# TensorE's program written out for all heads of attention and mLSTM, and the mLSTM key turns set one projection unit ahead of their products

## What is computed

```python
kw = kc * wk
C_new = decay[..., None, None] * C + jnp.einsum('bshd,bshe->bhde', kw, vc)
n_new = decay[..., None] * n + jnp.sum(kw, axis=1)
```

## Time and profile before

| | |
|---|---|
| median of 3 runs | 3012.46 us (3005.94 to 3017.71) |
| the profiled execution | 3015.32 us, of it the span 3013.5 us |
| PE busy | 2774.6 us, 92% of the span, 16995 matmuls |
| DVE, ACT, POOL busy | 42%, 27%, 22% |
| attention phase on PE | about 124 to 1231 us |
| output projection of layer 0 | about 1246 to 1510 us |
| mLSTM heads | about 1512 to 2809 us, some 161 us each |
| final output | about 2813 us to the end |

### The profile page before, as it was taken

The page is one execution under the profiler, slowest core; times in us unless marked ns, Lnnn a source line. Parts: engine busy times, 40 slices in busy tenths (PEclk is TensorE's granted clock), DMA queues, the critical chain, the costliest instruction groups (busy, mean ns, idle before and its releaser), DMA issues. The chain is left out here.

```text
span 3013.5 us, 49037 instructions
## 1 busy us (share of the span) xinstructions
PE 2774.6 (92%) x16995; PEld 2349.4 (78%) x16995; DVE 1270.0 (42%) x3433; ACT 815.0 (27%) x2119; POOL 657.3 (22%) x815
## 2 busy tenths in 40 slices
PE   6789989999999899799799999999999999999898
PEld 3577777868777777588588888888889898888687
DVE  3536545472636365555403333241514142424633
ACT  3314423250524143222312212131313121222111
POOL 2421021103011211343101212030303031212532
PEclk9899999999999999799899999999999999999999
DMA  9411020203011111244102222121303121314443
GB/s 359 163 44 51 8 87 12 58 9 89 2 58 52 46 48 47 88 139 133 62 23 39 76 34 74 34 80 17 94 18 76 38 69 39 61 53 118 148 143 109
DMA packets 186555, 217.95 MB, mean 72 GB/s; under 512 B 26288, under 2 KB 133248, under 8 KB 184400
## 3 DMA queue, kind: packets, MB, share of 16 engines
q1 hardware_dynamic: 176336, 187.37, 21.7%
q10 hardware_dynamic: 9984, 27.37, 2.4%
HBM read 176.64 MB, written 38.07 MB: 71 GB/s over the span
## 5 line engine op out<-in xcount | busy, mean ns | idle before, releaser
L501 PE MATMUL psum<-h_hi,mlstm_w_lo 128*128 128x384 f32 (+1 forms) x1600 | 610.9, 382 | 33.6 <-issue 20.8
L502 PE MATMUL psum<-h_lo,mlstm_w_hi 128*128 128x384 f32 (+1 forms) x1600 | 579.2, 362 | 0.0
L503 PE MATMUL psum<-h_hi,mlstm_w_hi 128*128 128x384 f32 (+1 forms) x1600 | 578.3, 361 | 0.0
L501 PEld LDWEIGHTS psum<-h_hi,mlstm_w_lo 128*128 128x128 f32 x1600 | 305.4, 191 | 60.9 <-issue 31.7
L503 PEld LDWEIGHTS psum<-h_hi,mlstm_w_hi 128*128 128x128 f32 x1600 | 304.2, 190 | 28.8
L502 PEld LDWEIGHTS psum<-h_lo,mlstm_w_hi 128*128 128x128 f32 x1600 | 305.6, 191 | 21.0
L501 PE MATMUL psum<-h_hi,attn_w_lo 128*128 128x384 f32 (+1 forms) x800 | 293.8, 367 | 27.2 <-DVEq L779 12.3
L502 PE MATMUL psum<-h_lo,attn_w_hi 128*128 128x384 f32 (+1 forms) x800 | 290.6, 363 | 0.0
L503 PE MATMUL psum<-h_hi,attn_w_hi 128*128 128x384 f32 (+1 forms) x800 | 290.0, 362 | 0.0
L470 POOL CAST mlstm_w_hi<-mlstm_w_raw 128x512 fp32r<-128x512 f32 x78 | 47.9, 614 | 823.1 <-PE psum L503 757.5
L751 ACT ACTIVATE arena<-arena,negm 128x640 f32<-128x640 f32 (+2 forms) x208 | 161.8, 778 | 218.2 <-DVE negm L836 218.2
(11 more groups left out here) (276 smaller groups left out, 4898.4 us busy)
## 6 DMA issues: line engine op xcount, KB each, us to landing
m_bc<-gate_rows_mlstm SPq DMA_DIRECT2D x128, 256.0 KB, 3.8
mlstm_w_raw<-in_mlstm_w_in SPq DMA_DIRECT2D x40, 512.0 KB, 4.8
h_full<-gated_output SPq DMA_DIRECT2D x31, 512.0 KB, 4.1
arena<-in_rotary SPq DMA_DIRECT2D x24, 512.0 KB, 6.9
arena<-in_rotary SPq DMA_DIRECT2D x24, 384.0 KB, 3.7
gated_output<-gT SPq DMA_DIRECT2D x8, 1088.0 KB, 5.2
layer_output<-xb_out ACTq DMA_DIRECT2D x17, 512.0 KB, 2.6
h_hi_full<-layer_output SPq DMA_DIRECT2D x17, 512.0 KB, 4.7
```

Of the source, the lines that this page charges most:

```text
L501: pe.matmul(out, self.lo[:, k, :], E.h_hi[:, k, tok], start=(k == 0), stop=False)
L502: pe.matmul(out, self.hi[:, k, :], E.h_lo[:, k, tok], start=False, stop=False)
L503: ins = pe.matmul(out, self.hi[:, k, :], E.h_hi[:, k, tok], start=False, stop=(k == KT - 1))
```

## The change

Three things. TensorE's program for attention and for mLSTM is written out for all heads, so that no branch back and no wait against a register is left in it; the other engines keep their loops. The turn of a key tile and its products are put one projection unit apart: after unit i TensorE makes the products of tiles 2i-2 and 2i-1 and then turns tiles 2i and 2i+1, and ACT's copies follow in that order. And the two waits between the key units and the first query unit go behind that unit.

```diff
             def _(pe):
-                with pe.Fori(0, NKV) as kv:
+                for kv in range(NKV):
                     for m, kind in enumerate(kinds):
...
                         evac(NG + i)
-                        for c in (2 * i - 1, 2 * i):
+                        for c in (2 * i - 2, 2 * i - 1):
                             if 0 <= c < NT:
                                 act.wait_ge(s_kv, at(h * NT + c + 1))
...
-                    def key_step(s):
-
-                        if s < NT:
-                            if s >= 2:
-                                pe.wait_ge(s_kw, at(h * NT + s - 1))
-                            pe.transpose(E.bank[4 + s % 2][:, 0:P], kT[:, s * P:(s + 1) * P], E.ident[:, :]).then_inc(s_kT, 1)
-                        c = s - 1
-                        if 0 <= c < NT:
-                            pe.wait_ge(s_kw, at(h * NT + c + 1))
-                            if c >= 2:
-                                pe.wait_ge(s_kvb, at(h * NT + c - 1))
-                            for d in range(2):
-                                ins = pe.matmul(E.bank[6 + c % 2][:, d * E1:(d + 1) * E1], kw[c % 2][:, d, :],
-                                                v1[:, c, :], start=True, stop=True, skip_group_check=True)
-                            ins.then_inc(s_kv, 1)
+                    def key_turn(s):
+                        if s >= NT:
+                            return
+                        if s >= 2:
+                            pe.wait_ge(s_kw, at(h * NT + s - 1))
+                        pe.transpose(E.bank[4 + s % 2][:, 0:P], kT[:, s * P:(s + 1) * P], E.ident[:, :]).then_inc(s_kT, 1)
+
+                    def key_products(c):
+                        if not 0 <= c < NT:
+                            return
+                        pe.wait_ge(s_kw, at(h * NT + c + 1))
+                        if c >= 2:
+                            pe.wait_ge(s_kvb, at(h * NT + c - 1))
+                        for d in range(2):
+                            ins = pe.matmul(E.bank[6 + c % 2][:, d * E1:(d + 1) * E1], kw[c % 2][:, d, :],
+                                            v1[:, c, :], start=True, stop=True, skip_group_check=True)
+                        ins.then_inc(s_kv, 1)
...
                     for u in range(1, NG):
                         unit(u)
-                    pe.wait_ge(s_relA, at(h * NA + NG))
-                    pe.wait_ge(s_og, at(h * NT))
                     for i in range(NA):
                         unit(NG + i)
                         if i == 0:
+                            pe.wait_ge(s_relA, at(h * NA + NG))
+                            pe.wait_ge(s_og, at(h * NT))
                             pe.wait_ge(s_v1, at(h * NG + NG))
-                        key_step(2 * i)
-                        key_step(2 * i + 1)
+                        key_products(2 * i - 2)
+                        key_products(2 * i - 1)
+                        key_turn(2 * i)
+                        key_turn(2 * i + 1)
                     pe.wait_ge(s_relA, at(h * NA + NA))
...
-                all_heads(pe, MH, head)
+                for h in range(MH):
+                    head(h, h == MH - 1)
                 F.pe(pe)
```

## The result

The median of the changed kernel is 2935.5 us (2930.7 to 2941.8, four runs) against 3013.1 (3005.9 to 3017.7, four runs): a ratio of 0.9746, 95% interval 0.9719 to 0.9773, so 77.6 us or 2.5% faster. 2935 with a range of 2917 to 2959 had been said.

What follows compares the result with a forecast made beforehand. The prediction took PE, busy 92% of the span, as the bound. Its terms, 24.7 + 15.6 - 0.9 + 7.3 + 32.6 - 1.5 = 77.8 us, off 3012.5 gave 2935 us, range 2917 to 2959.

Steps and rivals of the forecast that it cites:

- A, passages of mLSTM: Six mLSTM passages between heads, 68.0 us with branches back, fall to 7.21 us each written out: 24.7 us saved.
- B, first units in attention: Three branches back in attention: the pauses go and each first unit falls to 5.59 us, 15.6 us saved.
- C, waits moved: Between mLSTM's key and query units, two waits go behind the first query unit: 7.3 us saved.
- D, keys apart: mLSTM key steps, turns and products one unit apart: 4.07 us saved a head, 32.6 in all.
- row loads later, head 7: Gate row loads in mLSTM head 7 meet the output weights' transfer: 1.5 us lost, bounds 0 and 5.
- rotary tables late in attention: In attention DVE and POOL start late against PE, then catch up: 0.9 us lost, bounds 0 and 5.
- E, register waits: Removing register waits in attention's blocks saves 0, bounds 0 and 12 us.
- Only the listed stalls go: Key steps keep their short pauses as product pairs still wait for semaphores: 18.7 us less saved, 2953 us; chance 0.12.
- Slow matmuls stay: At the passages the shorter pauses still cost the matmul rate: 18.1 us less saved, 2953 us; chance 0.07.
- Gate rows last: Late row loads make ACT and PE wait at the start of every head's steps: 35 us, 2970 us; chance 0.05.
- The branch is not paid for: Pauses at passages are waits for weights or semaphores and stay; branch removal gives about 1 us: 2973 us; chance 0.03.
- Straight code is fetched late: A program without loops finds each of some 148 instruction packets late: 136 us added, 3071 us; chance 0.03.

Runs made afterwards that it cites:

- e2: The kernel before with only TensorE's mLSTM program written out: 2987.6 us, ratio 0.9932.
- e4: The kernel before with only the two waits moved behind the first query unit: 3000.6 us, ratio 0.9972.
- e3: The kernel before with only key turns and products one unit apart (ACT's copies following), loops and the two waits kept: 2979.4 us, ratio 0.9904.
- e1: The kernel before with only TensorE's attention program written out: 2989.4 us, ratio 0.9935.
- e6: The changed kernel with TensorE loops of two heads a trip, one branch back in attention and two in mLSTM: 2947.1 us, ratio 0.9784.
- e7: The changed kernel with SP loading the second q projection's first two rotary tables ahead of the next weights: 2930.9 us, ratio 0.9722.
- e9: The changed kernel with rotary tables ahead of weights in attention and half the next key weights' low part early in mLSTM: 2923.4 us, ratio 0.9710.
- e10: e9 with ACT, not POOL, casting the high part of the gates' weights in attention: 2915.9 us, ratio 0.9681.
- e5: The changed kernel with each written-out TensorE head in a one-trip device loop, its branch never taken; waits folded to constants: 2934.2 us, ratio 0.9739.

## Why the prediction was right

**The size and its parts.** 77.8 us had been summed and 77.6 were measured. Term by term, by the traces:

| step | predicted | measured |
|---|---|---|
| A, passages of mLSTM | 7.21 us each | 7.22 each, seven alike; e2 alone 23.6 (24.7) |
| B, first units in attention | no pause, 5.59 us | no pause, 5.52 to 5.57 |
| C, waits moved | 7.3 | 1.10 us became 0.17: 7.2; e4 alone 10.6 (5 to 11 by the ratio) |
| D, keys apart | 4.07 us a head | 4.03 a head (14.48 to 10.45); e3 alone 31.8 (32.6) |
| a head of mLSTM | 152 us | 152.3 |
| row loads later, head 7 | -1.5 | line 2044 waits 8.8 us there, 7.8 before: -1.0 |
| rotary tables late in attention | -0.9 | new pauses -3.3, not in e1; the rest varies by trace |
| E, register waits | 0 (0 to 12) | some 3 to 4 |

**That the sum fits to 0.2 us is luck.** The interval of the ratio is 68 to 85 us, and the largest terms were read from one trace. The six passages came to 68.0 us there; in e1, e3 and e4, which keep the branches, they come to 65.2, 64.7 and 62.6, so the mean of four traces gives 21.8 us for part A and not 24.7. The three first units of part B took 22.7 us there and 21.5 in e2, e3 and e4. What stands is the mechanism of each part, shown alone by e1 to e4, and the size to some us.

**Two smaller terms were mis-sized, in opposite directions.** The first is part E, which I put at 0 because the key intervals of head 7 equal those of head 6. That holds for the key steps (e3), but not for the blocks of attention: less the pauses at the branches they take 581.2 to 583.2 us in the five traces with register waits (before, e2, e3, e4, e6) and 577.0 to 579.3 in the eight without. Of the 20.6 us that e1 saves in attention the pauses are 9.8, the three slow units 5.2, the blocks 3.4 and the steps behind the keys' projection 1.8, but those steps are not shorter in the other traces without register waits. The bounds of 0 and 12 held it; the choice of the lower end, from the rows of another phase, was the error. No run has the register waits and no taken branch, so the 3 to 4 us go by this comparison.

The second is the sentence that DVE and POOL "catch up over five units", 0.3 us a head. In three of the four heads of the changed kernel they have not caught up at the second projection of gates, where POOL's cast stands behind its last rotary product; that costs 3.3 us against before. e7, e9 and e10, which change that order, have no such pause. But e1, with the branches gone in attention too, has none either, so what puts the tables late enough in the changed kernel stays open. I had named a new entry for line 486 before line 501 as a sign of being wrong: in attention it came (5.3 to 9.1 us), small enough to leave the sum standing.

**The rivals.** "Only the listed stalls go" gives 13.9 us for e3, which gave 31.8 (21 to 36 by the ratio): out. "Slow matmuls stay": passages of 7.22 us: out. "Gate rows last": line 2044 gained 1.0 us in all, and the first wait of the steps in each head is 0.95 as before: out. "The branch is not paid for" needed A and B at 1 us, and e1 and e2 gave 21.9 and 23.6: out. "Straight code is fetched late": no pause at regular distances, and 137 packets: out. I had said some 148; each branch back took two to three packets of its own (148 in e1 without three branches, 146 in e2 without six and in e6 with three).

The Trainium skill (Advanced Engine Details and Errata, Control Flow Timing) has about 108 ns for a compare-and-branch; by that figure e5's eleven would be 1.2 us, an estimate, and too little for the times to tell. Its trace doesn't have it on PE's path: 0.25, 0.23 and 0.23 us at the ends of attention's body, with the branch and without. The Trainium skill (Runtime: NRT & Kernel Launch, Instruction fetch mechanics) says that a taken branch out of the fetched window waits for its target page; e6 agrees, with 3.1 to 3.5 us of "issue" at each of three. The 81 ns for a matmul of 128 columns with its weight load in the Trainium skill (TensorE: Matmul & The Clock Gate, Back-to-back issue gap) is not what this form shows: line 1986 with its eight matmuls and two turns takes 1.20 us between projection matmuls, and part D gave 32, not 44.

## What to carry to other kernels

Compare a looped passage with one that falls through, from the last matmul before to the first after the next unit: that difference, idle and slow matmuls together, is what writing out gives, and it came out to 0.01 us for a passage. But read the looped ones in several traces, or allow for their spread: six took 62.6 to 68.0 us. Keep dependent steps on the bounding engine one unit apart where, as here, the unit (4 to 5.4 us) is longer than the other engine's turn. When the bounding engine gets faster at the head of a phase, look at what else stands in order before the operand it needs next (here a cast behind a rotary product, a table behind a weight load, a half of the weights behind a gate): those orders were worth 19 us more.

## What the hardware showed

- A taken branch back of PE costs 3.1 to 3.7 us of pause (39 of them in six traces), the same for a body of one head and of two. Behind 38 of them the granted clock falls to 0.50 for a while, and 24 matmuls of 512 columns take 6.9 to 8.5 us instead of 5.55. Eleven branches that aren't taken cost nothing measurable (0.23 to 0.25 us from body to body, with them and without).
- How long one pause is doesn't settle by itself what the clock does. Behind the 1.36 us at the passages and the 1.86 us in attention the granted clock stays at 1.00 (the 0.23 us steps above). Behind one branch back in e4, a pause of 3.44 us, it stays at 1.00 too, and the unit takes 5.61 us. And at the second pair of a head in the kernel before, the same waits of 1.17 and 1.70 us are followed by a clock of 1.00 once (329 to 335 us) and of 0.55 another time (605 to 611 us).
- Register waits go with 3 to 4 us more in attention's blocks (581.2 to 583.2 us against 577.0 to 579.3), whose operations are short and many, and with nothing in the key steps of mLSTM (10.6 us a head in both forms).
- DVE's subtraction takes 0.69 us for a half of the weights alone, and 1.06 beside POOL's cast in the changed kernel; before, the cast was the one that took longer, 0.91 us where it takes 0.61 alone.
